# A decoder block with 32 experts on one core: first halves of expert weights sent behind the next expert's other pieces, from expert 16 on

## The chip, the cores and the metric

The kernel runs on one core of a Trainium2 chip. The metric is device time in microseconds (us); the kernel before took 1587.29 us, the median of three runs (1586.08 to 1588.47).

## The reference, cut to what matters

The block has two parts: a mixer (attention and a recurrence, with one input and one output projection), and a mixture of 32 SwiGLU experts. The change touches only the experts. All weights are float32.

```python
x = x + gt1 * rmsnorm(hybrid_mixer(h, ...), g_post_mix)
h = rmsnorm(x, g_pre_ffn) * (1 + sc2) + sh2            # 256 tokens, 2048 wide
for gi in range(4):                                    # 4 groups of 8 experts
    hid = silu(h @ w_gate[gi]) * (h @ w_up[gi])        # each 2048 x 512
    y = y + (hid * cw[:, gi, :, None]) @ w_down[gi]    # 512 x 2048; cw is 0 where a token isn't routed
x = x + gt2 * rmsnorm(y, g_post_ffn)
```

Every expert has 12.6 MB of weights (gate, up and down, 4.2 MB each), and all 32 are read once, whatever the routing.

## The kernel before

**Work of an expert.** The tokens of an expert (up to 64) are gathered with a matmul against a one-hot matrix, two experts at a time; gate and up are computed side by side in bank 0 over 16 steps of the contraction (k = 0 to 15); ScalarE and VectorE form the hidden values; four small transposes follow; the down product goes over four steps; and the results of two experts are scattered back with matmuls and added up by VectorE. A branch for tokens beyond 64 for an expert is passed over here.

**Pieces.** The weights of expert e come in six transfers of 2 MB, called (e,0) to (e,5) below: 0 and 1 are the first halves of gate and up (used in k = 0 to 7), 2 and 3 their second halves (k = 8 to 15), 4 and 5 the halves of down. They are issued by SyncE (SP in the profile), in program order, on one DMA queue. Slots 0 to 5 of the tile `ring` hold them; the first halves of odd experts go to two more places instead, the tiles RT and RH. So first halves have room for two experts, and pieces 2 to 5 for one.

**Freeing.** TensorE (PE) counts up `expert_used` six times for each expert: after the last matmul on pieces 0 and 1 (k = 7), on pieces 2 and 3 (k = 15), and on each half of down. SyncE waits for these counts before it overwrites a slot. `first_halves(e, q)` waits for counts 1 and 2 of expert e and sends (e+2,0) and (e+2,1) (line L498); `next_piece(e + 1, s, e)` waits for count s+1 of expert e and sends (e+1,s) (line L503). SyncE waits in order, so a wait holds up all that is written behind it.

**TensorE's lines.** L1129 is the gate and up product (64 instructions for an expert, 32 for either half), L1162 the down product (32). Between them stand, for an even expert, the scatter of the pair before (L1044, in two parts) and four transposes (L1148); for an odd one the gather of the next pair (L1025), the transposes of the weighted one-hot matrix (L1144) and the four transposes. The last expert, 31, has its own code: L1055 for gate and up (64 instructions, one piece after another), L1065 its transposes, L1076 for down, L1091 for the last scatter. In L1076 the first 8 of 32 instructions need only (31,4); the ninth waits for (31,5).

**Before the experts.** The mixer's weights pass through the same `ring` and end before about 620 us; expert 1's waits are then served from 640 us on.

Of the kernel before, what the change touches and what calls it, by code (L numbers as in the profile page):

```python
# [87 lines left out]
TRANSFERS = [[2 if name[0] == "head" else 1 for name in names] for names in SLOT_LOADS]  # L88
PLACE = {name: (slot, n) for slot, names in enumerate(SLOT_LOADS) for n, name in enumerate(names)}
HEAD_TILES = 15  # L90
CHUNKS = [(0, 4), (4, 4), (8, 4), (12, 2), (14, 2)]
BY_DVE = [k0 + i for k0, n in CHUNKS for i in range(n // 2)]
BY_ACT = [k0 + i for k0, n in CHUNKS for i in range(n // 2, n)]
HEAD_COL = COL_HQ + 128
# [61 lines left out]
class Lane:  # L156
# [8 lines left out]
    def do(self, ins, sig=None):  # L165
        sig = sig or self.own
        ins.then_inc(sig.sem, 1)
        sig.n = sig.n + 1
        self.last = (sig, sig.n)
# [6 lines left out]
def block_kernel(nc, a, out):  # L176
# [3 lines left out]
    with ExitStack() as ctx:  # L180
# [5 lines left out]
        def sig(name):  # L186

            if name in STAGE_OF:
                stages, n = STAGE_OF[name]
                counted = sig(stages)  # L190
                assert counted.n == n - 1, name
                return counted
            if name not in sems:
                sems[name] = Signal(ctx.enter_context(nc.semaphore(name)))
            return sems[name]

        def wait(eng, name, n=1):

            if name in STAGE_OF:
                name, n = STAGE_OF[name]  # L200
            eng.wait_ge(sig(name).sem, n)
# [119 lines left out]
        def landed(eng, name):  # L321

            s, n = PLACE[name]
            eng.wait_ge(sig(f"landed{s}").sem, 16 * sum(TRANSFERS[s][0:n + 1]))
# [21 lines left out]
        def rows_of(name, k, n):  # L346
            return flat(name)[:, 0:k * n].rearrange("p (k c) -> p k c", k=k)
# [3 lines left out]
        def _(sp):  # L351
            def send(name, src):

                s, n = PLACE[name]
                if n:
                    sp.wait_ge(sig(f"freed{s}").sem, n)
                sp.dma_start(rows_of(name, src.shape[1], src.shape[2]), src).then_inc(sig(f"landed{s}").sem, 16)
# [8 lines left out]
            def head(c, r):  # L366

                s, n = PLACE[("head", c, r)]
                k0, w = CHUNKS[c][0], CHUNKS[c][1] * P
                if n:  # L370
# [8 lines left out]
            def first(q, h):  # L379
                send(("first", q, h), win_k[:, 4 * q + 2 * h:4 * q + 2 * h + 2, HEAD_COL:HEAD_COL + HEAD_TILES * P])  # L380

# [90 lines left out]
            def expert_halves(e):  # L472
                g, u, d = (w[bass.ds(e, 1)].rearrange("o p x -> p (o x)") for w in (wg, wu, wd))
                return [g[:, 0:4096], u[:, 0:4096], g[:, 4096:8192], u[:, 4096:8192], d[:, 0:4096], d[:, 4096:8192]]

            def dst_of(s):
                return ring[:, s, :, :].rearrange("p a b -> p (a b)")
# [14 lines left out]
            def first_halves(e, q):  # L492

                pieces = expert_halves(e + 2)
                for s in range(2):
                    sp.wait_ge(sig("expert_used").sem, e * HB + (s + 1))
                    dst, name = (odd[s], f"odd_landed{s}") if q else (dst_of(s), f"expert_landed{s}")
                    sp.dma_start(dst, pieces[s]).then_inc(sig(name).sem, 16)  # L498

            def next_piece(e, s, used_of):  # L500

                sp.wait_ge(sig("expert_used").sem, used_of * HB + (s + 1))
                sp.dma_start(dst_of(s), expert_halves(e)[s]).then_inc(sig(f"expert_landed{s}").sem, 16)  # L503
# [6 lines left out]
            for s in range(3, HB):  # L510
                next_piece(2, s, 1)
            for e in range(2, NE - 2):
                first_halves(e, e % 2)
                for s in range(2, HB):
                    next_piece(e + 1, s, e)
            for s in range(2, HB):
                next_piece(NE - 1, s, NE - 2)

# [22 lines left out]
        def _(pe):  # L541
# [37 lines left out]
            def head_columns(c):  # L579

                k0, n = CHUNKS[c]
                if c > 0:
# [31 lines left out]
            for c in range(5):  # L614
                k0, nk = CHUNKS[c]
                for k in range(k0, k0 + nk):
# [5 lines left out]
                    if k % 2 == 0:  # L622
                        landed(pe, ("first", q, h))
                    w = rows_of(("first", q, h), 2, HEAD_TILES * P)
                    tiles = list(range(HEAD_TILES))
                    if k == KT - 1:
                        tiles = tiles[7:] + tiles[:7]
                    for n, t in enumerate(tiles):
                        if c < 4 and k == k0 + nk - 1 and n == (8, 8, 1, 8)[c]:
# [3 lines left out]
                                  start=k == 0 and (t == 0 or t % 2 == 1), stop=k == KT - 1, skip_group_check=True)  # L633
                        if k == KT - 1 and t == HEAD_TILES - 1:
                            last.then_inc(sig("forget_full").sem, 1)
# [584 lines left out]
        def _(act):  # L1220
# [27 lines left out]
            do(fn(wide[:, 0:BLK], bank[5][:, :], ACT.Copy), sig("shift_row"))  # L1248
            for c, (k0, nk) in enumerate(CHUNKS):
                wait(act, "column_sums", c + 1)  # L1250
# [1020 lines left out]
```

## Time and profile before

| | |
|---|---|
| median of three runs | 1587.29 us |
| the profiled execution's own time | 1579.64 us |
| its span | 1577.4 us |
| TensorE busy, share of the span | 1519.5 us, 96% |
| VectorE, ScalarE, GpSimd busy | 43%, 15%, 3% |
| DMA, mean over the span | 374 GB/s, 589.96 MB |
| granted TensorE clock, mean | 0.996 |

The span is the time from the first to the last instruction. The profiled execution took 7.65 us less than the median of the timed runs. TensorE's busy time counts matmuls that overlap in its pipeline, and their ends are modelled, so a share of 96% doesn't say by itself that TensorE is the limit.

### The profile page before, as it was taken

What the parts mean: (1) busy time and instruction counts of PE and PEld (TensorE: products, weight loads), DVE (VectorE), ACT (ScalarE), POOL (GpSimd) and SP (SyncE); (2) the same over time, 40 slices, a digit from 0 to 9 for tenths busy, and PEclk for the clock granted to TensorE, in tenths of its full rate; (3) what the DMA queues carried; (4) which work ended last, traced back from release to release, by engine and by line L of the source; (5) the groups of instructions that cost most, each with busy time, mean ns of one, the idle gap of its engine ahead of it and who ended that gap; (6) DMA issues with size and microseconds to landing.
All of it is one profiled execution on the core that took longest, in us unless ns stands there. A gap on an engine that the chain in (4) does not pass through costs nothing.

```text
span 1577.4 us, 19275 instructions
## 1 busy us (share of the span) xinstructions
PE 1519.5 (96%) x8012; PEld 819.4 (52%) x8012; DVE 679.8 (43%) x1223; ACT 232.8 (15%) x445; POOL 40.7 (3%) x57
## 2 busy tenths in 40 slices
PE   4999999999999999999999999999999999999996
PEld 2988888855554447344344434434434434434432
DVE  3564767776787635232232232332332332322325
ACT  2100311121232303011011011010010010010003
POOL 2000000000001200000000000000000000000002
PEclk9999999999999999999999999999999999999998
DMA  9999577799778996799999999999999999999992
GB/s 359 398 385 372 223 259 283 271 360 353 274 290 307 366 404 252 321 427 428 429 428 429 428 429 427 428 428 428 429 428 429 428 429 428 429 428 429 427 406 82
DMA packets 102322, 589.96 MB, mean 374 GB/s; under 512 B 5744, under 2 KB 16464, under 8 KB 76928
## 3 DMA queue, kind: packets, MB, share of 16 engines
q1 hardware_dynamic: 99904, 580.93, 90.7%
q0 software_dynamic: 1696, 5.66, 1.0%
q10 hardware_dynamic: 672, 2.66, 0.5%
q8 instruction: 36, 0.59, 0.2%
q14 instruction: 14, 0.11, 0.0%
HBM read 587.07 MB, written 2.16 MB: 374 GB/s over the span
## 4 chain that ended last, share of the span: by engine, by line
PE 55%; DMA 35%; SPq 5%; DVE 3%; issue 1%; ACT 0%; ACTq 0%; DVEq 0%
DMA ring<-in_w_up 32%; PE bank L1129 17%; PE bank L914 7%; PE bank L666 5%; SPq L376 4%; PE bank L1162 4%; PE bank L632 3%; PE bank L857 3%; PE bank L1025 2%; DMA ring<-in_w_ada 2%; PE bank L700 2%; PE bank L1044 2%; PE bank L679 1%; PE bank L682 1%; DMA ring<-in_w_in 1%; PE bank L1055 1%
## 5 line engine op out<-in xcount | busy, mean ns | idle before, releaser
L1129 PE MATMUL bank<-ring,RN 128*64 128x512 f32 x1488 | 331.7, 594 | 13.5 <-DMA ring<-in_w_up 13.4
L1129 PEld LDWEIGHTS bank<-ring,RN 128*64 128x64 f32 x1488 | 106.0, 137 | 228.8 <-issue 195.8
L1162 PE MATMUL bank<-ring,RN 128*64 128x512 f32 x992 | 219.7, 595 | 0.5 <-issue 0.5
L2150 DVE TENSOR_TENSOR RN<-bank,RN 64x512 f32<-64x512 f32 x31 | 21.5, 693 | 381.4 <-ACT RN L1482 381.4
L1162 PEld LDWEIGHTS bank<-ring,RN 128*64 128x64 f32 x992 | 68.9, 137 | 137.4 <-issue 135.6
L2157 DVE COPY RG<-bank 64x512 f32<-64x512 f32 x64 | 44.1, 689 | 196.1 <-PE bank L1162 188.4
L1025 PEld LDWEIGHTS bank<-RN,RX 128*128 128x128 f32 x1024 | 117.0, 192 | 13.0 <-issue 13.0
L1025 PE MATMUL bank<-RN,RX 128*128 128x128 f32 x1024 | 121.2, 277 | 0.0
L1129 PE MATMUL bank<-RT,RN 128*64 128x512 f32 x256 | 112.3, 592 | 0.0
L914 PE MATMUL bank<-ring,RT 128*128 128x512 f32 x256 | 111.3, 594 | 0.8 <-DVE RT L1964 0.8
L1044 PE MATMUL bank<-RG,RN 128*128 128x512 f32 x240 | 109.5, 599 | 0.0
L2085 DVE TENSOR_SCALAR RN<-bank,aff 128x128 f32<-128x128 f32 x256 | 87.5, 405 | 45.0 <-PE bank L1025 45.0
L1129 PE MATMUL bank<-RH,RN 128*64 128x512 f32 x240 | 105.4, 592 | 0.0
L2123 DVE TENSOR_TENSOR RT<-RT,bank 128x512 f32<-128x512 f32 x112 | 75.8, 687 | 20.5 <-PE bank L1044 18.5
L666 PE MATMUL bank<-RH,ring 128*128 128x256 f32 x384 | 84.0, 380 | 0.0
L1673 DVE SCALAR_TENSOR_TENSOR wide<-ring,silv,wide 128x1024 f32<-128x1024 f32 x60 | 77.0, 1284 | 8.2 <-DMA ring<-in_w_ada 6.5
L914 PEld LDWEIGHTS bank<-ring,RT 128*128 128x128 f32 x256 | 48.2, 190 | 60.6 <-issue 59.6
L666 PEld LDWEIGHTS bank<-RH,ring 128*128 128x128 f32 x384 | 72.6, 190 | 9.9
L1482 ACT ACTIVATE RN<-bank 64x512 f32<-64x512 f32 x31 | 18.3, 589 | 399.2 <-PE bank L1129 399.2
L1496 ACT ACTIVATE RG<-bank 64x512 f32<-64x512 f32 x64 | 37.9, 592 | 263.8 <-PE bank L1162 259.1
L1129 PEld LDWEIGHTS bank<-RT,RN 128*64 128x64 f32 x256 | 35.1, 137 | 72.1 <-issue 72.1
L1044 PEld LDWEIGHTS bank<-RG,RN 128*128 128x128 f32 x240 | 43.4, 191 | 55.2 <-issue 51.6
(386 smaller groups left out, 1475.1 us busy)
## 6 DMA issues: line engine op xcount, KB each, us to landing
ring<-in_w_down SPq DMA_DIRECT2D x64, 2048.0 KB, 16.0
ring<-in_w_up SPq DMA_DIRECT2D x48, 2048.0 KB, 20.2
ring<-in_w_gate SPq DMA_DIRECT2D x47, 2048.0 KB, 17.3
ring<-in_w_ada SPq DMA_DIRECT2D x32, 2048.0 KB, 10.6
ring<-in_w_in SPq DMA_DIRECT2D x18, 2048.0 KB, 9.2
RT<-in_w_gate SPq DMA_DIRECT2D x17, 2048.0 KB, 15.5
RH<-in_w_up SPq DMA_DIRECT2D x16, 2048.0 KB, 20.0
ring<-in_w_ada SPq DMA_DIRECT2D x18, 1024.0 KB, 18.2
```

The costliest lines, as they stand in the source:

```text
L376: sp.dma_start(dst[:, j0:j1, m * w:(m + 1) * w], ada_k[:, 4 * r + j0:4 * r + j1, m * D + k0 * P:m * D + k0 * P + w]).then_inc(sig(landing) ...
L632: last = mm(half_, w[:, k % 2, t * P:(t + 1) * P], hT[:, k, :], start=k == 0 and (t == 0 or t % 2 == 1), stop=k == KT - 1, skip_group_chec ...
L666: last = mm(bank[PAIR[name][m // 2]][:, (m % 2) * S:(m % 2 + 1) * S], w[:, m * P:(m + 1) * P], hT[:, k, :], start=k == 0 and m % 2 == 0, s ...
L857: last = mm(bank[2][:, :], hT[:, k, tt * P:(tt + 1) * P], rows_of((name, k // 8), 8, BLK)[:, k % 8, :], start=k == 0, stop=k == KT - 1)
L914: last = mm(bank[OUT_BANKS[n][tt]][:, :], mixed(k)[:, tt * P:(tt + 1) * P], rows_of(("out", n, h), 8, BLK)[:, k % 8, :], start=k == 0, sto ...
L1025: last = mm(bank[GB[m % 3]][:, (k % 4) * P:(k % 4 + 1) * P], x_t[:, tt, k * P:(k + 1) * P], onehot[:, tt, :], start=tt == 0, stop=tt == TT ...
L1044: mm(bank[4 + i % 4][:, :], ohwT[:, tt * P:(tt + 1) * P], rows[:, c * BLK:(c + 1) * BLK], start=True, stop=True).then_inc(sig("scattered") ...
L1129: last = mm(bank[0][64 * s:64 * s + 64, :], tokT[:, k, q * CAP:(q + 1) * CAP], w[:, k % 8, :], start=k == 0, stop=k == KT - 1, skip_group_ ...
L1162: last = mm(bank[2 + n % 2][64 * (n // 2):64 * (n // 2) + 64, :], hidT[:, k * CAP:(k + 1) * CAP], wdn[:, n * BLK:(n + 1) * BLK], start=k = ...
L1673: ins = stt(acc_w, w[:, k, :], c, acc_w, ALU.mult, ALU.add)
L2085: ins = ts(tokT[:, k, :], bank[GB[m % 3]][:, (k % 4) * P:(k % 4 + 1) * P], aff[:, 2, k:k + 1], aff[:, 3, k:k + 1], ALU.mult, ALU.add)
L2123: ins = v.tensor_copy(w, bank[4 + i % 4][:, :]) if first else tt_op(w, w, bank[4 + i % 4][:, :], ALU.add)
```

## The change

From e = 16 on, SyncE's loop sends pieces 2 to 5 of expert e+1 first and the first halves of expert e+2 after them. No transfer is added, removed or resized; all waits and destinations stay as they are.

```diff
+IN_ORDER = 16
...
             for e in range(2, NE - 2):
-                first_halves(e, e % 2)
+                if e < IN_ORDER:
+                    first_halves(e, e % 2)
                 for s in range(2, HB):
                     next_piece(e + 1, s, e)
+                if e >= IN_ORDER:
+                    first_halves(e, e % 2)
             for s in range(2, HB):
                 next_piece(NE - 1, s, NE - 2)
```

## Rows read from the trace of the kernel before

**Rows 1.** The page, part 2: GB/s moved in 40 equal slices of the span.

```profile
GB/s 359 398 385 372 223 259 283 271 360 353 274 290 307 366 404 252 321 427 428 429 428 429 428 429 427 428 428 428 429 428 429 428 429 428 429 428 429 427 406 82
```

**Rows 2.** Stretches: busy us of PE, PEld, DVE, ACT, POOL; clock, DMA share, GB/s.

```profile
700.00:843.30 143.30, 143.30 (x687) 60.58 (x684) 42.29 (x91) 14.38 (x25) 0.00 (x0) 1.00 1.01 428
...
931.00:1490.00 559.00, 547.27 (x2666) 234.33 (x2666) 161.06 (x358) 56.46 (x95) 0.00 (x0) 1.00 1.01 429
```

**Rows 3.** The chain that ended last, 655 to 745 us: start, us, what.

```profile
657.99 13.73 PE bank L1129 x64
...
679.77 7.02 PE bank L1162 x32
686.79 13.73 PE bank L1129 x64
...
715.07 13.73 PE bank L1129 x64
```

**Rows 4.** The chain that ended last, 1080 to 1135 us.

```profile
1077.98 21.84 DMA ring<-in_w_up
...
1099.87 7.14 PE bank L1129 x32
...
1107.35 21.83 DMA ring<-in_w_up
```

**Rows 5.** SyncE in order of time, 1090 to 1165 us: start, us, issue, count.

```profile
1106.98 0.33 SPq L503 DMA_DIRECT2D ring<-in_w_gate  x1
...
1118.12 3.76 SPq L503 DMA_DIRECT2D ring<-in_w_down  x2
1128.40 0.33 SPq L498 DMA_DIRECT2D RT<-in_w_gate  x1
```

**Rows 6.** The chain that ended last, 1480 us to the end.

```profile
1489.09 21.84 DMA ring<-in_w_up
...
1511.07 7.09 PE bank L1129 x32
...
1525.69 7.02 PE bank L1162 x32
1532.70 13.76 PE bank L1055 x64
...
1549.03 7.09 PE bank L1076 x32
```

**Rows 7.** SyncE in order of time, 1495 us to the end.

```profile
1500.36 3.76 SPq L503 DMA_DIRECT2D ring<-in_w_down  x2
1518.15 0.33 SPq L503 DMA_DIRECT2D ring<-in_w_gate  x1
1518.52 0.43 SPq L503 DMA_DIRECT2D ring<-in_w_up  x1
1529.31 3.76 SPq L503 DMA_DIRECT2D ring<-in_w_down  x2
```

**Rows 8.** Single issues, last number us to landing: at 1503.79, 1518.15, 1518.52, 1529.31, 1532.74.

```profile
ring<-in_w_down SPq DMA_DIRECT2D x1, 2048.0 KB, 16.9
...
ring<-in_w_gate SPq DMA_DIRECT2D x1, 2048.0 KB, 7.6
...
ring<-in_w_up SPq DMA_DIRECT2D x1, 2048.0 KB, 12.1
...
ring<-in_w_down SPq DMA_DIRECT2D x1, 2048.0 KB, 7.3
...
ring<-in_w_down SPq DMA_DIRECT2D x1, 2048.0 KB, 10.3
```

**Rows 9.** DMA rates around the last down pieces; columns as in rows 2.

```profile
1527.00:1529.50 2.50, 2.50 (x14) 0.82 (x12) 0.00 (x0) 0.00 (x0) 0.00 (x0) 1.00 0.98 419
1529.50:1530.50 1.00, 1.00 (x8) 0.40 (x6) 0.00 (x0) 0.00 (x0) 0.00 (x0) 1.00 0.93 197
1530.50:1531.50 1.00, 1.00 (x8) 0.32 (x6) 0.00 (x0) 0.00 (x0) 0.00 (x0) 1.00 0.26 82
1531.50:1535.00 3.50, 3.50 (x18) 1.15 (x16) 1.38 (x2) 1.19 (x2) 0.00 (x0) 1.00 1.06 445
...
1540.50:1542.00 1.50, 1.50 (x10) 0.45 (x8) 1.50 (x2) 0.00 (x0) 0.00 (x0) 1.00 0.08 33
```

**Rows 10.** DMA queues from 1538 to 1539 us: packets, MB, share of 16 engines.

```profile
q8 instruction: 1, 0.02, 5.7%
```

## The prediction, made before the changed kernel ran

> **What bounds the kernel now.** I read the page's rate line first [rows 1]: from the 18th slice, about 670 us, to the 38th the DMA engines move 427 to 429 GB/s without a break. Below that ceiling lie the mixer and the tail, which the change doesn't touch. A flat line at a ceiling says that the queue is never empty; it doesn't say who waits. For that I read the stretches [rows 2] and the chain.
>
> In the early stretch TensorE is busy throughout (143.30 of 143.30 us) [rows 2], and the chain holds only TensorE: two experts take from 657.99 to 715.07 us, 57.08 us, or 28.54 us each [rows 3]. The DMA queue runs full too, but with pieces sent ahead. Later the chain changes [rows 4]: in each expert it goes through the landing of piece 3, the second half of up. TensorE's second half begins at 1099.87 us for expert 16 and at 1511.07 for expert 30 [rows 4, 6], 14 experts and 411.20 us later: 29.37 us each. Six transfers of 2 MB in 29.37 us is 4.894 us a transfer, which is the ceiling again. So the stream needs 29.37 us for an expert, TensorE 28.54; the lead of the early experts is used up and TensorE waits some 0.8 us in each expert. The stream is the limit, and rows 2 of the late stretch show it (TensorE 547.27 of 559.00 us, DMA at 429 GB/s).
>
> The end is different. After (30,3) lands at 1489.09 + 21.84 = 1510.93 us [rows 6] nothing on the chain waits for a transfer any more: TensorE runs the rest of expert 30, expert 31 and the last scatter. The end of the kernel is the landing of (30,3) plus 66.5 us of compute. What counts is how early in the stream (30,3) comes.
>
> **The change part by part.** *What it moves.* Before, the stream's order near the end is (31,0) (31,1) (30,2) (30,3) (30,4) (30,5) (31,2) to (31,5). After it is (30,2) (30,3) (30,4) (30,5) (31,0) (31,1) (31,2) to (31,5). The two first halves move from ahead of (30,3) to behind it. With a full queue (30,3) then lands two transfers sooner: 2 x 4.894 = 9.79 us. The bytes are the same, 192 transfers in all, and so is the place of (31,2) to (31,5).
>
> *What is queued behind the moved step.* SyncE now waits for the end of expert e's down before it issues (e+2,0) and (e+2,1). Two issues follow one another in under 1 us, and nothing else stands on SyncE's queue. Once the stream sets the pace, the end of down(e) comes some 21.7 to 22.2 us after (e,3) lands, and (e+2,0) begins in the stream some 39 us after it: no delay. (e+1,1) lands 2 x 4.894 = 9.8 us ahead of (e+1,3), so 19.6 us after (e,3); TensorE turns to expert e+1 at 21.7 us. First halves are in time by about 2 us.
>
> *The switch, experts 16 to 18.* Here a cost arises. Behind (16,4) and (16,5) the two transfers (18,0) and (18,1) are gone, so the queue holds two where it held four. I lay it out from the landing of (16,3) at 1099.82 us. (16,5) lands at 1109.6. (17,2) and (17,3) are issued at 1106.98 and 1107.35 [rows 5], 2.6 us ahead of that; (17,4) at 1118.12 [rows 5], some 1.3 us ahead of the landing of (17,3) at about 1119.5. The trace has the same case already, at its end, where nothing follows (30,5): (30,5) lands at 1503.79 + 16.9 = 1520.69, (31,2) is issued 2.54 us before and lands at 1525.75, 5.06 us after it (0.17 over a transfer); (31,3) lands at 1530.62; (31,4) is issued 1.31 us before that and lands at 1536.61, 5.99 us after (1.09 over a transfer) [rows 7, 8]. The rate falls to 197 and then 82 GB/s for a microsecond each [rows 9]: the queue has run dry and starts again. So the switch costs 0.17 + 1.09 = 1.26 us, once.
>
> The next experts: (17,4) lands at about 1125.5, and from there (18,3) at 1150. TensorE, now fed ahead, runs at its own pace: expert 17 from 1121.5, its down begins near 1143.3 and frees slot 4 near 1146.9. (18,4) is thus issued 3.1 us ahead of the landing of (18,3), above the 2.54 us that cost 0.17. For (19,4) it is about 4.2 us, and the lead grows as TensorE gains 0.83 us an expert on the stream. One dry spell, then none. Even a longer restart is paid once, since it moves the stream back against TensorE.
>
> *Can TensorE follow?* (30,3) now lands at 1510.93 - 9.79 + 1.26 = 1502.40 us. TensorE at its own pace reaches the second half of expert 30 at 1099.87 + 7 x 57.08 = 1499.43 us. It has caught up 3 us before, near expert 27, and the stream is again what it waits for. Gain so far 8.53 us.
>
> *The tail.* TensorE's needs move up by 8.53 us, the landings of (31,2) to (31,5) don't. (31,3), at 1530.62 + 1.26 = 1531.9, is needed by the last quarter of L1055, at 1532.70 + 0.75 x 13.76 - 8.53 = 1534.5: in time. (31,4), no longer behind a dry queue, comes near 1536.7 and is needed at 1540.5: in time. (31,5): the ninth instruction of L1076 stands at 1549.03 - 8.53 + 8 x 7.09/32 = 1542.27. Before, (31,5) landed at 1532.74 + 10.3 = 1543.04 [rows 8], 6.4 us after (31,4), 1.5 us over a transfer: from 1540.5 to 1542 only 33 GB/s flow [rows 9], one engine finishing late, and a 16 KB block of instructions passed on one engine shortly before [rows 10]. After, the count of transfers gives 1510.93 + 6 x 4.894 + 1.26 = 1541.55, and with the same late engine 1543.05. So TensorE waits 0 to 0.78 us for a piece that nobody waited for before. I take 0.78, because the block of instructions will be fetched in the new kernel as well.
>
> The Trainium skill, in "Runtime: NRT & Kernel Launch", section "Instruction fetch mechanics", says that the engines fetch instructions in 16 KiB blocks by themselves and that this is mostly hidden. By that rule (31,5) would land at 1541.55, TensorE would not wait, and the gain would be 8.53 us and not 7.75; the size of the block in the trace agrees, the late landing beside it speaks against the rule here. The skill's "DMA: Bandwidth & Descriptors", "Anatomy of one DMA — SWDGE (gpsimd) path", gives a fixed cost of about 2.0 us beside bytes over 436 GB/s, for the other issue path; as an estimate a lone transfer would land after 6.8 us, where the trace has 7.3, and the restart would cost 0.6 us and not 1.09. Both keep the sum within 1 us.
>
> *Sum.* -9.79 + 1.26 + 0.78 = -7.75 us. Against the profiled execution: span 1577.4 to about 1569.6, own time 1579.64 to 1571.9. The timed runs lie 7.65 us above the profiled one, and no view says where; I take the same difference off their median: 1587.29 - 7.75 = 1579.5 us. If those 7.65 us lie in the transfers (0.7% on each), the terms hardly change: 0.04 us more a transfer makes the first term 9.86 and moves (31,5) by 0.2.
>
> **Bounds.** Restart: 0 (the queue doesn't run dry) to 2.75 us (1.26 and the 1.5 us of the late engine, if that belongs to the restart and not to the block of instructions). Wait for (31,5): 0 to 2.3 us (0.78 and once more 1.5). Gain 4.7 to 9.8 us, 1577.5 to 1582.6.
>
> **Rivals.** *The stream's end binds more than I think (same).* The end can't come sooner than (31,5) plus its compute: from 1543.04 to the 1550.8 us at which it was needed are 7.8 us of slack. If a transfer takes longer on the timed runs, this slack shrinks by six times the excess. At 5.66 us a transfer the gain is down to 3.2 us, at 6.2 us it is nothing: 1584.1 to 1587.3. The late stretch's 429 GB/s speaks against it. 0.08.
>
> *TensorE doesn't catch up (faster, but less).* The landing of (30,3) then doesn't count. The gain is 14 x (29.37 - pace): at 28.54 there are 11.6 us, at 29.0 only 5.2, giving 1582. The early stretch ran at 28.54 beside a full stream [rows 2, 3], which speaks against it. With further dry spells at experts 18 and 19 counted here, 0.13.
>
> *(31,5) is in time, or the queue doesn't run dry (faster, more).* With the restart, but without the late engine, L1076 doesn't wait and the gain is 8.53 us: 1578.8. If the queue doesn't run dry either, 9 to 9.8 us: 1577.5 to 1578.3. For the first, an instruction block can fall on an engine that is ahead and then costs nothing; against the second, the same leads cost 1.26 us at the end of this trace. 0.22 together, most of it the first, which is also what the Trainium skill's rule on instruction fetch would give.
>
> *The new order makes the transfers slower (slower).* Place: all 84 transfers of experts 17 to 30. The order of reads over gate, up and down changes, and the first halves' slots are written next to the second halves'. It decides at 9.79/84 = 0.117 us a transfer (2.4%), where the gain is gone; at 0.155 us (3.2%) the kernel is 3.2 us slower, about 1590.5. The early and late stretches, with TensorE's reads at quite different points of the stream, differ by 428 to 429 GB/s, so the rate doesn't seem to care. 0.04.
>
> *The order does nothing (same).* If waits and not order set the landings, (30,3) lands where it did: 1587.3. The queue holds more than four transfers when (30,3) is issued (21.84 us to land against 7.3 alone), which speaks against it. 0.03.
>
> **How the numbers follow.** My case (gain 6.5 to 8.2 us, 1579.1 to 1580.8) has 0.50. Faster by over 0.2% (3.2 us, about what a measurement of this kernel can tell from no change) are my case, the one above it and the partial one: 0.50 + 0.22 + 0.13 = 0.85. Within 0.2%: 0.08 + 0.03 = 0.11. Slower 0.04. The range 1577.3 to 1583.6 holds my case, the better one and nearly all of the partial one: about 0.83.
>
> **What the profile after would show.** The chain: in experts 17 to about 26 TensorE alone, at 57.1 us for two; from about 27 to 30 the landing of piece 3 again. (30,3) landing near 1502.4 us. SyncE: (17,4) issued near 1118.1 and landing some 7.3 us later, the rate down for about 2 us around 1119; (18,4) landing without such a spell. The last L1076 starting near 1540.5 and waiting up to 1 us after its eighth instruction for the down piece, which lands near 1543. The rate line otherwise at 428. The prediction would be wrong if the rate falls in several experts after the switch, if TensorE waits for piece 1, or if L1076 waits several microseconds.

## The result, and the profile after

The changed kernel took 1572.91 us (median of four runs, 1571.26 to 1578.25) against 1587.57 us for the kernel before in the same timing (four runs, 1586.08 to 1588.47): ratio 0.9922, 95% interval 0.9893 to 0.9951. The forecast was 1579.5 us with a range from 1577.3 to 1583.6, so the measured time lies below the range. A second, longer timing (the first experiment below) gave 1575.31 against 1583.43 us, ratio 0.9947 (0.9930 to 0.9965). That is a gain of 8.1 us by the medians, where 7.75 were forecast; the time itself lies below the range here too. In that timing one of 33 executions of the kernel before took 4129.75 us, and one of the 12 of e2_order_before 7474.58 us; both are left out of every comparison below.

The profiled execution of the changed kernel took 1578.25 us, its span 1576.0, only 1.4 us less than the span before. The new file is four lines longer at TensorE's lines (L1129 is L1133 here, L1162 is L1166, L1076 is L1080, L1091 is L1095) and one at SyncE's (L503 is L504, L498 is L499).

**The switch.** The chain of the changed kernel around expert 16 (start us, us, what), to be set beside [rows 4]:

```profile
1084.42 21.83 DMA ring<-in_w_up
1106.29 7.09 PE bank L1133 x32
1113.38 5.35 PE bank L1048 x12
...
1127.93 13.73 PE bank L1133 x64
...
1156.72 13.73 PE bank L1133 x64
```

Expert 16's second half starts at 1106.29 us. From there up to expert 26 no landing is on the chain, and expert 18 starts 28.79 us after expert 17: TensorE runs at its own pace. SyncE's order around it, beside [rows 5]:

```profile
1113.40 0.33 SPq L504 DMA_DIRECT2D ring<-in_w_gate  x1
1113.77 0.43 SPq L504 DMA_DIRECT2D ring<-in_w_up  x1
1124.54 3.76 SPq L504 DMA_DIRECT2D ring<-in_w_down  x2
1128.34 0.43 SPq L499 DMA_DIRECT2D ring<-in_w_gate  x1
1128.82 0.45 SPq L499 DMA_DIRECT2D ring<-in_w_up  x1
```

Single issues of the same stretch, the last number us to landing, for those at 1113.77, 1124.54, 1127.97 and 1128.34 us:

```profile
ring<-in_w_up SPq DMA_DIRECT2D x1, 2048.0 KB, 12.1
...
ring<-in_w_down SPq DMA_DIRECT2D x1, 2048.0 KB, 7.2
...
ring<-in_w_down SPq DMA_DIRECT2D x1, 2048.0 KB, 8.6
...
ring<-in_w_gate SPq DMA_DIRECT2D x1, 2048.0 KB, 13.2
```

(Landings are read to 0.1 us.) (17,2) lands at 1120.9, 4.9 us after (16,5): the 0.17 us forecast for it doesn't show. (17,3) lands at 1125.87 and (17,4) at 1131.74, 5.87 us later: 0.98 us over a transfer, where 1.09 had been read from [rows 7, 8]. (17,5) follows after 4.8 us, so the 1.5 us of the late engine don't belong to a restart. The rate shows the same gap (start and end of a stretch, its length, busy us of PE, PEld, DVE, ACT, POOL; clock, DMA share, GB/s), and over the 328 us from 1158 us on it is full:

```profile
1123.00:1125.00 2.00, 2.00 (x12) 0.72 (x10) 0.00 (x0) 0.00 (x0) 0.00 (x0) 1.00 0.83 352
1125.00:1126.00 1.00, 1.00 (x6) 0.29 (x4) 0.00 (x0) 0.00 (x0) 0.00 (x0) 1.00 1.04 213
1126.00:1127.00 1.00, 1.00 (x8) 0.39 (x6) 0.00 (x0) 0.00 (x0) 0.00 (x0) 1.00 0.69 262
...
1158.00:1486.00 328.00, 326.38 (x1586) 138.73 (x1580) 93.96 (x210) 33.28 (x55) 0.00 (x0) 1.00 1.01 428
```

**The end.** The chain of the changed kernel from expert 26 to the last scatter, beside [rows 6]:

```profile
1385.04 13.78 PE bank L1133 x64
1398.82 0.30 SPq L504
1399.17 21.35 DMA ring<-in_w_up
1420.56 7.14 PE bank L1133 x32
...
1486.82 21.84 DMA ring<-in_w_up
1508.66 0.14 issue
1508.80 7.09 PE bank L1133 x32
...
1530.48 18.80 DMA ring<-in_w_down
1549.28 0.04 issue
1549.32 5.37 PE bank L1080 x24
```

The landing of piece 3 is back on the chain for expert 27, as forecast. Expert 30's second half starts at 1508.80 us, 402.51 us after expert 16's; before it was 411.20 us. That is 8.69 us, where 8.53 were forecast. The last down product then stops after its eighth instruction and waits for the last piece until 1549.28 us. TensorE alone in the order of time shows how long:

```profile
1546.77 1.94 PE L1080 MATMUL bank<-ring,RN 128*64 128x512 f32 x8 [0.31 <-issue]
1549.32 5.37 PE L1080 MATMUL bank<-ring,RN 128*64 128x512 f32 x24 [0.62 <-DMA ring<-in_w_down]
```

The ninth instruction starts 2.55 us after the first; unhindered it would start after 1.77 us. The wait is 0.78 us, the very number forecast, though the lateness behind it arose at another transfer than the prediction had it (see the account of the prediction below). From expert 16's second half to the end of the span it is 469.7 us against 477.5: 7.8 us gained.

**Where the profiled span lost them again.** The changed kernel's expert 2 starts its 64 gate and up instructions at 664.58 us; before that was 657.99 us [rows 3]. These 6.6 us arise long before the first instruction that the change touches. Some 1.5 us are spread over the mixer. The rest stands in two stretches, 3.4 us in the first and 1.7 us in the second, here for the changed kernel; the last three numbers are the granted clock, DMA share and GB/s:

```profile
600.00:605.00 5.00, 4.60 (x42) 4.39 (x41) 1.46 (x6) 2.85 (x8) 0.00 (x0) 1.00 0.97 360
605.00:611.00 6.00, 6.00 (x15) 3.42 (x15) 3.19 (x19) 0.00 (x0) 0.00 (x0) 0.50 0.12 49
...
656.00:660.00 4.00, 4.00 (x12) 1.39 (x10) 0.00 (x0) 0.00 (x0) 0.00 (x0) 0.57 1.07 455
```

The granted clock is at 0.50, 1.2 and not 2.4 GHz, in the last steps of the output projection and again around the down product just ahead of expert 2. Ahead of the first lies a stretch in which TensorE runs small instructions with short pauses (4.60 of 5 us busy). e2_order_before below has the same stretch (4.59 of 5 us) and keeps its clock, so the pauses alone don't explain it.

### The profile page after: what moved, and what is told of

Read it like the earlier page. It is cut to its first block, busy times and chain, and to the rows that moved or that the text cites. A ratio compares the mean times of both kernels' runs of the same rounds, so it can differ in the third digit from the quotient of the medians.

```text
span 1576.0 us, 19275 instructions
## 1 busy us (share of the span) xinstructions
PE 1524.1 (97%) x8012; PEld 823.6 (52%) x8012; DVE 679.5 (43%) x1223; ACT 232.5 (15%) x445; POOL 40.6 (3%) x57
## 4 chain that ended last, share of the span: by engine, by line
PE 72%; DMA 21%; DVE 3%; SPq 3%; issue 1%; ACT 0%; ACTq 0%; DVEq 0%
PE bank L1133 22%; DMA ring<-in_w_up 17%; PE bank L1166 9%; PE bank L918 7%; PE bank L670 5%; PE bank L636 5%; PE bank L1029 5%; PE bank L1048 4%; PE bank L861 4%; SPq L377 2%; DMA ring<-in_w_ada 2%; PE bank L704 2%; PE bank L683 1%; PE bank L686 1%; DMA ring<-in_w_down 1%; DMA ring<-in_w_in 1%
## 5 line engine op out<-in xcount | busy, mean ns | idle before, releaser
L1133 PE MATMUL bank<-ring,RN 128*64 128x512 f32 x1488 | 330.1, 593 | 7.0 <-DMA ring<-in_w_up 7.0
L1166 PE MATMUL bank<-ring,RN 128*64 128x512 f32 x992 | 221.4, 599 | 0.5 <-issue 0.5
L1133 PEld LDWEIGHTS bank<-ring,RN 128*64 128x64 f32 x1488 | 106.9, 137 | 219.1 <-issue 201.3
L1166 PEld LDWEIGHTS bank<-ring,RN 128*64 128x64 f32 x992 | 69.4, 137 | 138.5 <-issue 136.7
L1133 PE MATMUL bank<-RT,RN 128*64 128x512 f32 x256 | 112.3, 592 | 0.0
L1133 PE MATMUL bank<-RH,RN 128*64 128x512 f32 x240 | 105.4, 592 | 0.0
L1133 PEld LDWEIGHTS bank<-RT,RN 128*64 128x64 f32 x256 | 35.1, 137 | 72.1 <-issue 72.1
## 6 DMA issues: line engine op xcount, KB each, us to landing
ring<-in_w_up SPq DMA_DIRECT2D x48, 2048.0 KB, 19.5
```

Source lines behind the costliest of these rows:

```text
L1133: last = mm(bank[0][64 * s:64 * s + 64, :], tokT[:, k, q * CAP:(q + 1) * CAP], w[:, k % 8, :], start=k == 0, stop=k == KT - 1, skip_group_ ...
L1166: last = mm(bank[2 + n % 2][64 * (n // 2):64 * (n // 2) + 64, :], hidT[:, k * CAP:(k + 1) * CAP], wdn[:, n * BLK:(n + 1) * BLK], start=k = ...
```

## The experiments

Two theories stood against each other after the first timing. Theory A: the change is worth its forecast 7.8 us, and the rest of the 14.7 us is chance of the executions. Theory B: the change itself is worth 14.7 us. The others test single steps of the sum.

**e1_again: the changed kernel once more.** No edit.

> The changed kernel once more, against the kernel before. Its profile and that of before agree from the landing of (16,3) on within 0.2 us with what was forecast (8.7 us sooner at (30,3), 0.8 us lost at (31,5)), so theory A says: the change is worth 7.8 us, ratio 0.9951, and the other 7 us of the first timing are stretches at half the granted TensorE clock ahead of the experts, which come and go with the execution; here the medians differ by 5 to 11 us, and executions with the same clock by about 8. Theory B says that the change itself is worth about 14.7 us in undisturbed executions (ratio 0.990 to 0.992 again, at equal clocks too), by something in the expert part that the one profile doesn't show.

Measured: 1575.31 us (10 runs, 1572.01 to 1580.72) against 1583.43 us, ratio 0.9947 (0.9930 to 0.9965). Theory B's ratio of 0.9922 is outside. Each kernel spreads over 8 us: that of before from 1579.61 to 1587.75 us. The spread goes with the mean granted clock. The kernel before, over this timing and that of e5_between to e8_split: 1579.7 us mean at clock 0.996 (3 runs), 1581.3 at 0.993 and 0.994 (21 runs), 1585.1 at 0.992 (12), 1586.4 at 0.991 (12); one run at 0.995 and two at 0.990 make up the rest. The changed kernel here: 1572.3 at 0.993 and 0.994 (3 runs), 1575.5 at 0.992 (3), 1578.2 at 0.991 (2). At equal clocks the difference is 8 to 10 us. The four runs of the changed kernel in the first timing fit this too: 1578.25 us at 0.991, 1572.86 and 1572.96 at 0.993 and 1571.26 at 0.995 lie 8.2 to 8.4 us under the kernel before at the same clock (1586.4, 1581.3, and 1579.6 for its one run at 0.995). The first timing's runs of before all lay at the upper end of its spread, and three of four of the changed kernel at the lower end of its own. Theory B falls.

In this execution's profile (30,3) took 22.98 us to land and not 21.84, and the last down product did not wait. That is not because the last piece came sooner: (31,5) landed 442.9 us after expert 16's second half, where it was 443.0 in the first profile. TensorE came 1.2 us later to expert 30's second half (403.71 and not 402.51 us). The tail's terms vary by a microsecond, their sum less: 470.2 us from expert 16's second half to the end. This profile also has the low clock, 0.50 from 605 to 611 us.

**e2_order_before: the same file, the order of before.**

```diff
-IN_ORDER = 16
+IN_ORDER = 30
```

> The changed file with the switch at expert 30, which issues the same instructions in the order of the kernel before. Theory A and B: no difference by the order, ratio 1.000. If executions differ by chance in their clock, its median can still lie some microseconds off that of before (A: within 0.997 to 1.003); a third theory, that the file or its load and not the order makes the difference, expects it near the changed kernel, 0.992.

Measured: 1582.39 against 1583.43 us, ratio 0.9996 (0.9980 to 1.0011). Neither the file nor its load makes the difference. In its profile the two distances are 411.22 and 477.5 us, those of before to 0.1 us. The granted clock stays at 1.00 from 605 to 611 us, and expert 2 starts at 658.33:

```profile
605.00:611.00 6.00, 6.00 (x15) 2.66 (x14) 3.02 (x19) 0.00 (x0) 0.00 (x0) 1.00 0.00 0
```

**e3_from24: the switch eight experts later.**

```diff
-IN_ORDER = 16
+IN_ORDER = 24
```

> The switch at expert 24 and not 16. If TensorE has to catch up at its own pace (28.54 us an expert against 29.37), only 6 experts are left for it: 3 x 1.65 = 4.9 us sooner at the second half of expert 30, TensorE and not the stream on the chain there, no wait for (31,5) in the last down product: gain 4.9 us, ratio 0.9969. If the place of (30,3) in the stream alone decides, the gain is that of the change: 7.8 us.

Measured: 1577.65 us, ratio 0.9970 (0.9956 to 0.9985). Its chain has no landing any more over the last experts (the view ends at 1552 us, one instruction before the end of the last down product):

```profile
1500.42 13.73 PE bank L1133 x64
...
1528.71 13.76 PE bank L1059 x64
...
1545.04 7.05 PE bank L1080 x31
```

From expert 16's second half (1100.91 us) to the end of its span (1573.4) it is 472.5 us: 5.0 us gained, 4.9 expected. The gain is what TensorE can catch up. The place of (30,3) in the stream alone doesn't decide.

**e4_from29: one step alone.**

```diff
-IN_ORDER = 16
+IN_ORDER = 29
```

> Only expert 29's step in the new order: (31,0) and (31,1) behind (30,2) to (30,5), one expert for TensorE to catch up. Catch-up theory: at most 0.8 us gained, ratio 0.9995, within the noise; (30,3) lands about 9.8 us sooner and waits for TensorE. Place-in-the-stream theory: 7 to 8 us, ratio 0.995.

Measured: 1582.69 us, ratio 0.9993 (0.9979 to 1.0007). SyncE's issues of (30,2) and (30,3) in its profile, and the time to landing of (30,3):

```profile
1496.15 0.33 SPq L504 DMA_DIRECT2D ring<-in_w_gate  x1
1496.52 0.43 SPq L504 DMA_DIRECT2D ring<-in_w_up  x1
```

```profile
ring<-in_w_up SPq DMA_DIRECT2D x1, 2048.0 KB, 12.0
```

(30,3) lands at 1508.5 us, 19.5 us or four transfers after (29,3), where it took six before. TensorE reaches it only at 1518 us. From expert 16's second half to the end: 476.8 us, 0.7 us gained. This shows in one place that the piece comes two transfers sooner, and that this alone buys only the 0.7 us that TensorE can catch up in one expert. The profile also has the low clock ahead of the experts (0.52 from 605 to 611 us, expert 2 at 665.10 us), with the order of before up to expert 29: the low clock doesn't come from the new order.

**e5_between: the switch without the dry queue.** For experts 16 to 19 the first halves stand behind piece 3.

```diff
                 for s in range(2, HB):
+                    if s == 4 and IN_ORDER <= e < IN_ORDER + 4:
+                        first_halves(e, e % 2)
                     next_piece(e + 1, s, e)
-                if e >= IN_ORDER:
+                if e >= IN_ORDER + 4:
                     first_halves(e, e % 2)
```

> As the changed kernel, but in the steps of experts 16 to 19 the two first halves go between the pieces 3 and 4 of the next expert, not behind piece 5; from expert 20 on the order is that of the changed kernel. Dry-spell theory: (17,4) is now issued some 10 us ahead of its turn, so the 1.1 us gap in the rate at the switch is gone; (30,3) lands 9.5 to 9.8 us sooner than before (8.7 for the changed kernel), (31,5) some 1 us earlier, gain 8.8 against 7.8 us. Rival: the gap moves on to (18,4) or (e,4) becomes late for the down product (turn 14.7 us after (e,3), need 14.6), and nothing is gained over the changed kernel.

Measured: 1576.54 us (8 runs), ratio 0.9957 (0.9940 to 0.9974). This timing can't tell it from the changed kernel. In its profile the gap at (17,4) is gone: it is issued at 1121.92 us, 11 us ahead of its turn, and lands 4.8 us after the transfer ahead of it.

```profile
1120.00:1123.00 3.00, 3.00 (x17) 1.00 (x15) 0.00 (x0) 0.00 (x0) 0.00 (x0) 1.00 1.00 426
1123.00:1126.00 3.00, 3.00 (x17) 1.00 (x15) 0.64 (x1) 0.63 (x2) 0.00 (x0) 1.00 1.02 437
1126.00:1130.00 4.00, 4.00 (x22) 1.43 (x20) 1.62 (x6) 0.55 (x1) 0.00 (x0) 1.00 0.94 401
```

Expert 30's second half starts 401.76 us after expert 16's, 9.44 us less than before and 0.75 us less than in the changed kernel. Two places are worth 9.79 us, of which the changed kernel lacks 1.10; with the dry queue 0.75 of them go. The last down product didn't wait, and the end comes 468.1 us after expert 16's second half, 9.4 us sooner than before. The gap didn't move on either: from 1130 us to 1485 us the rate is 429 GB/s.

**e8_split: the changed kernel, the last piece in two.**

```diff
-            for s in range(2, HB):
+            for s in range(2, HB - 1):
                 next_piece(NE - 1, s, NE - 2)
+            sp.wait_ge(sig("expert_used").sem, (NE - 2) * HB + HB)
+            for r in range(2):
+                sp.dma_start(dst_of(5)[:, 2048 * r:2048 * (r + 1)],
+                             expert_halves(NE - 1)[5][:, 2048 * r:2048 * (r + 1)])\
+                    .then_inc(sig(("expert_landed5", "last_quarter")[r]).sem, 16)
...
+                        if b == 0 and k == 3:
+                            pe.wait_ge(sig("last_quarter").sem, 16)
```

> The changed kernel with only (31,5) split in two as in e6_between_split. The wait in the last down product (0.8 us in the changed kernel's profile) goes: 0 to 0.8 us less than the changed kernel, which the timing can hardly tell; the profile shows L1080's matmuls without an interval after the eighth. Gain 7.8 to 8.6 us, ratio 0.9948.

Measured: 1574.21 us, ratio 0.9940 (0.9921 to 0.9960). TensorE's last down product in its profile:

```profile
1543.70 7.19 PE L1086 MATMUL bank<-ring,RN 128*64 128x512 f32 x32 [0.31 <-issue]
```

It runs through in 7.19 us, where 7.09 is the undisturbed time. 469.4 us from expert 16's second half: 8.1 us gained. Here the split mattered: the first half lands at 1543.9 us, the second at 1546.4. The ninth instruction was due at 1545.47 us and the thirteenth at 1546.36. Had the ninth needed all of the piece and the piece landed when it did, it would have waited some 0.9 us. By the times alone the split can't be told: ratio 0.9940 against 0.9947.

**e6_between_split: both.** The edits of e5_between and e8_split.

> The kernel of e5_between, and (31,5) as two transfers of 1 MB, of which the ninth instruction of the last down product needs only the first and the thirteenth the second. If the last wait is for the end of the stream, the first half lands 2.4 us sooner, the wait of 0 to 0.8 us goes, and the gain is 9.3 to 9.6 us, ratio 0.994. If small transfers cost a start of their own, nothing or 0.5 us is lost.

Measured: 1576.07 us (6 runs), ratio 0.9947 (0.9926 to 0.9968). The profile has 468.5 us, a gain of 9.0, a little under the 9.3 to 9.6 expected, and no wait in the last down product. By time, e1_again, e5_between, e6_between_split and e8_split are one group; their intervals overlap.

**e7_all: the switch at expert 2.**

```diff
-IN_ORDER = 16
+IN_ORDER = 2
```

> The new order from expert 2 on. The stream sets the end by the place of (30,3) and by (31,5), wherever the switch lies as long as TensorE has time to catch up: gain as the changed kernel, 7.8 us, ratio 0.995. Against it: at expert 2 the queue is as short as TensorE's pace allows and the dry spells come in the first experts, where the stream is not yet full; each microsecond lost there is lost for good, since the stream runs without a gap to the end. If so the gain is 4 to 7 us.

Measured: 1580.22 us (12 runs), ratio 0.9976 (0.9962 to 0.9991): a gain of 3.3 us by the medians, so more than half of it is lost, and less is left than either expectation said (7.8 us, or 4 to 7). Its rates from 680 us on:

```profile
680.00:700.00 20.00, 20.00 (x127) 11.60 (x128) 8.53 (x23) 3.32 (x6) 0.00 (x0) 1.00 1.00 417
700.00:720.00 20.00, 20.00 (x80) 7.43 (x78) 6.13 (x9) 0.97 (x2) 0.00 (x0) 1.00 0.66 268
720.00:740.00 20.00, 20.00 (x109) 8.86 (x106) 4.42 (x11) 1.78 (x3) 0.00 (x0) 1.00 0.99 412
740.00:760.00 20.00, 20.00 (x113) 9.60 (x113) 6.46 (x18) 3.23 (x5) 0.00 (x0) 1.00 1.00 427
```

At 428 GB/s the first three stretches would have moved more by 0.5, 7.5 and 0.7 us of transfer. Here too the queue runs dry, and from 705 to 708 us nothing moves: so near the start TensorE's pace, not the stream's, sets when slots come free (no landing is on the chain from 655 to 725 us), and without the two first halves nothing is left to send. The stream is full from 740 us to the end, so the time is never won back: expert 30's second half starts 850.59 us after expert 2, before that was 853.08 us, so of the 9.79 us for two places 2.5 are left. From expert 2's start to the end its profile has 916.9 us, before 919.4, the changed kernel 911.4.

## Why the prediction was wrong, point by point

- **The bound and its place.** Right. In the kernel before the landing of piece 3 set the pace, and (30,3) set the end. e2_order_before shows the distances to 0.1 us with the order of before.
- **9.79 us for two places in the stream.** Right: e4_from29 shows the landing four and not six transfers after (29,3).
- **TensorE's catching up at 28.54 us an expert.** Right, and the step that makes the gain: 5.0 us with 6 experts left, 0.7 with one, and in the changed kernel the stream is back on the chain for expert 27, as named.
- **One dry spell, 1.26 us, once.** Right, a little too large: nothing at (17,2) for 0.17, 0.98 us at (17,4) for 1.09, and 8.69 us gained at (30,3) for 8.53. e5_between takes 0.75 us of it away. "Even a longer restart is paid once" holds at expert 16. In e7_all the loss stays between 680 and 740 us too, but it is several gaps in a row and costs most of the gain: a switch where TensorE sets the pace was not in the prediction.
- **The wait for (31,5), 0.78 us.** The size came out to 0.01 us, the path to it did not, so the exact match is in part luck. The prediction had (31,4) in time near 1536.7 us, 436.8 us after the start of expert 16's second half, and then (31,5) 1.5 us late. In the changed kernel's profile (31,4) landed after 438.2 us and (31,5) 4.8 us behind it, at the full rate. The time had been lost earlier: (30,4) landed 6.3 us after (30,3) and not 4.9, and at 1512 us, between the two, a 16 KB block of instructions passed. In e1_again such a block passed at 1505 us and (30,3) itself landed 6.1 us after (30,2). That the restart doesn't cause it is shown by (17,5).

  The block is the likely cause: from 1430 us to the landing of (31,5), in all ten profiles, every landing over 5.2 us behind the one before it has either a dry queue or such a block in between (7 of 20 blocks). But 13 blocks of the 20 passed without a delay, the second one of the changed kernel among them (1538 us), and no run takes the blocks away; so it is not shown, and why a block costs time in one place and none in another is open.

  The Trainium skill, in "Runtime: NRT & Kernel Launch", section "Instruction fetch mechanics", has the fetch mostly hidden. By that the prediction had (31,5) at 1541.55, which is 441.7 us after expert 16's second half; it landed after 443.0 and 442.9 us in the two profiles of the changed kernel. e1_again had no wait because TensorE came later, not because the rule held.
- **The time.** This step failed: "The timed runs lie 7.65 us above the profiled one, and no view says where; I take the same difference off their median", and with it a range that held no term for it. The 7.65 us are no constant. They lie within the spread of one and the same kernel, 1579.6 to 1588.5 us over all timings. The median of three given for before was from its upper end, the first timing of the changed kernel from its lower. Taken from the profiled execution (1579.64 at clock 0.996), 7.75 us less is 1571.9 us, near the three shorter runs of the changed kernel (1571.3 to 1573.0). The miss of 6.6 us adds up: 3.9 us by which 1587.29 lies above the kernel before in the long timing, 2.4 us by which 1572.91 lies below the changed kernel there, and 0.4 us between 8.1 and 7.75. The first two are chance of the executions, and only the last is the change.
- **The rivals.** Transfers don't get slower by the order (428 GB/s over 328 us); the stream's end didn't bind sooner than the 0.78 us above; the order does set the landings (e4_from29).

## What to carry to other kernels

Where a full stream of transfers limits and compute is only a little faster, the end is the landing of the last piece on the path plus the compute behind it. An order that puts this piece sooner pays only as far as compute can catch up, and costs a dry queue where it is switched if the issues hang on freed slots.

Before forecasting a time from a median of three, compare it with the profiled execution of the same kernel. If they differ by as much as the change is worth, that difference belongs into the range, and only ratios from a long paired timing, or distances between fixed places in two profiles, can tell the change.

## What the runs showed of the hardware

- The granted TensorE clock fell to 0.50 from 605 to 611 us in the changed kernel's profile and stayed at 1.00 there in that of the kernel before and of e2_order_before. All three run the same instructions up to there. Over the ten profiles expert 2 starts at 658.0 to 660.8 us where the clock stays at 1.00 in that stretch (five profiles), at 661.0 us where it is 0.72 (e8_split), and at 664.2 to 665.7 us where it is 0.50 to 0.59 (the changed kernel, e1_again, e4_from29, e7_all). That is most of the 8 us between executions, and slower runs have the lower mean clock (the groups under e1_again). Why one execution has these stretches and another not is open.
- A transfer of 2 MB issued 2.5 to 2.6 us ahead of its turn cost 0 to 0.2 us over the full rate, one issued 1.3 us ahead 1.0 to 1.1 us, in the middle of the changed kernel as at the end of the kernel before; one issued 0.7 us ahead cost 1.6 us ((30,4) in e4_from29). The lead is not all that counts: in e7_all a transfer issued at 691.12 us, 3.6 us ahead, still landed 1.3 us late, and the runs don't show why.
